# Norming inside the transposition: a diagonal tile of the tokens' factors in place of the identity

## What is computed

```
def rms_norm(x, gain):
    x32 = x.astype(jnp.float32)
    y = x32 * lax.rsqrt(jnp.mean(x32 * x32, axis=-1, keepdims=True) + RMS_EPS)
    return (y * gain.astype(jnp.float32)).astype(x.dtype)

mem_n = rms_norm(mem, mem_norm_gain)
for layer in range(DEPTH):
    hn = rms_norm(x, g[0]);  ...  x = x + rms_norm(y, g[1])
    y = memory_cross_attention(rms_norm(x, g[2]), mem_n, ...);  x = x + rms_norm(y, g[3])
    y = swiglu_ffn(rms_norm(x, g[4]), ...);  x = x + rms_norm(y, g[5])
```

## Time and profile before

| | us |
|---|---|
| median of three executions | 1306.91 |
| the profiled execution | 1306.6 |
| its span (first to last instruction) | 1304.8 |
| TensorE busy | 1286.3 (99%) |
| VectorE busy | 882.3 (68%) |
| ScalarE busy | 688.1 (53%) |
| GpSimd busy | 110.7 (8%) |

### The profile page before, as it was taken

How to read it: one execution, slowest core, us unless ns; L and a number is a source line. 1 busy time by engine, 2 the same in 40 slices (tenths; PEclk the granted TensorE clock), 3 DMA queues, 4 the chain that set the end, 5 groups by cost and what they waited for, 6 DMA issues and landing times.

```text
span 1304.8 us, 17684 instructions
## 1 busy us (share of the span) xinstructions
PE 1286.3 (99%) x7313; PEld 1108.8 (85%) x7313; DVE 882.3 (68%) x1035; ACT 688.1 (53%) x960; POOL 110.7 (8%) x176
## 2 busy tenths in 40 slices
PE   7999999999999999999999999999999999999999
PEld 6889897988888888888888888898877888888887
DVE  4566664776666767876576666768785566787775
ACT  4655554644444665564554444565556654654453
POOL 7200100100000100030100000101330003000000
PEclk9999999999999999999999999999999999999999
DMA  8754653555555543454355555553444445465552
GB/s 261 245 168 138 193 179 99 192 195 186 186 191 193 182 163 119 151 174 149 126 189 195 187 187 184 182 195 106 161 136 155 155 136 187 136 198 190 193 194 97
DMA packets 156113, 223.64 MB, mean 171 GB/s; under 512 B 6103, under 2 KB 107635, under 8 KB 156032
## 3 DMA queue, kind: packets, MB, share of 16 engines
q1 hardware_dynamic: 154240, 218.18, 50.1%
q0 software_dynamic: 1664, 4.27, 1.1%
q10 hardware_dynamic: 128, 0.05, 0.0%
HBM read 221.44 MB, written 1.05 MB: 171 GB/s over the span
## 4 chain that ended last, share of the span: by engine, by line
PE 91%; DVE 4%; ACT 3%; POOL 1%; issue 1%; DMA 1%; SPq 0%; POOLq 0%; ACTq 0%
PE ps L403 18%; PE ps L453 9%; PE ps L405 9%; PE ps L455 9%; PE ps L454 9%; PE ps L388 5%; PE ps L389 5%; PE ps L390 5%; PE ps L588 4%; PE ps L590 4%; PE ps L589 4%; DVE wlo L1671 1%; PE ps L475 1%; PE ps L901 1%; ACT whi L1131 1%; PE ps L523 1%
## 5 line engine op out<-in xcount | busy, mean ns | idle before, releaser
L1671 DVE TENSOR_TENSOR wlo<-raw,whi 128x1024 fp32r<-128x1024 f32 x411 | 493.0, 1229 | 171.2 <-ACT whi L1131 168.4
L1131 ACT ACTIVATE whi<-raw 128x1024 fp32r<-128x1024 f32 x412 | 425.4, 1052 | 341.5 <-PE ps L403 156.1
L403 PE MATMUL ps<-RR,whi 128*128 128x512 f32 x1024 | 353.7, 396 | 0.7 <-DVE ar L1774 0.7
L405 PE MATMUL ps<-RR,wlo 128*128 128x256 f32 x1024 | 264.8, 279 | 0.1
L453 PE MATMUL ps<-whi,RR 128*128 128x512 f32 x592 | 238.0, 402 | 1.6 <-DVE RR L1945 0.4
L455 PE MATMUL ps<-whi,RR 128*128 128x512 f32 x592 | 231.0, 390 | 0.0
L454 PE MATMUL ps<-wlo,RR 128*128 128x512 f32 x592 | 230.9, 390 | 0.0
L403 PEld LDWEIGHTS ps<-RR,whi 128*128 128x128 f32 x1024 | 184.8, 188 | 36.3 <-DVE ar L1774 0.9
L405 PEld LDWEIGHTS ps<-RR,wlo 128*128 128x128 f32 x1024 | 193.0, 188 | 11.8 <-DVE RR L1701 0.4
L388 PE MATMUL ps<-RR,whi 128*128 128x256 f32 x512 | 147.4, 288 | 1.7 <-DVE RR L1701 1.3
L389 PE MATMUL ps<-RR,whi 128*128 128x256 f32 x512 | 144.8, 283 | 0.0
(11 more groups left out here) (337 smaller groups left out, 1275.4 us busy)
## 6 DMA issues: line engine op xcount, KB each, us to landing
raw<-in_ffn_w_gate_up SPq DMA_DIRECT2D x44, 1024.0 KB, 5.0
raw<-in_ffn_w_down SPq DMA_DIRECT2D x33, 1024.0 KB, 4.8
raw<-in_w_in SPq DMA_DIRECT2D x28, 1024.0 KB, 4.9
raw<-in_ffn_w_up SPq DMA_DIRECT2D x22, 1024.0 KB, 5.1
raw<-in_xa_w_kv SPq DMA_DIRECT2D x16, 1024.0 KB, 5.2
raw<-in_sb_w_qkv SPq DMA_DIRECT2D x12, 1024.0 KB, 5.0
raw<-in_ml_w_in SPq DMA_DIRECT2D x11, 1024.0 KB, 7.6
raw<-in_xa_w_q SPq DMA_DIRECT2D x8, 1024.0 KB, 5.3
```

Source lines behind the costliest of these rows:

```text
L403: m = pe.matmul(two(ps[:, bank, :]), p.hi[:, k, :], XT2[:, k, :, :], start=k == 0, stop=k == 7)
L405: pe.matmul(ps[:, bank, 0:256], p.lo[:, k, :], X.h[:, k, :], start=False, stop=False)
L1131: act.activation(p.hi, p.raw, ACT.Copy).then_inc(S["w_hi"], 1)
L1671: dve.tensor_tensor(p.lo, p.raw, p.hi.bitcast(F32), ALU.subtract).then_inc(S["w_lo"], 2 if p.n == 2 else 1)
```

## The change

The row tile is no longer multiplied. VectorE multiplies the 128 by 128 identity by the 128 factors of the row tile instead, which gives a diagonal tile `dg[:, t, :]`, in norms of tokens and of memory. TensorE then multiplies the raw rows (`xr`, or `mem_tm` for the memory) by that diagonal tile in a plain matmul: the result is the transposed block, each token's column scaled by its factor. The position of every instruction in every engine's program is the same; its operands, and on TensorE its kind, change. GpSimd's reload of `mem_tm` with the second memory now waits until the last low parts of the first memory's transposed rows are written, since TensorE reads `mem_tm` itself.

```diff
+        dg = sb("dg", [128, NT, 128])
...
+            def scaled_tile(src, t, k, b, half):
+
+                return pe.matmul(ps[:, b, 256 * half + 128 * t:256 * half + 128 * t + 128], src[:, t, 128 * k:128 * k + 128],
+                                 dg[:, t, :], start=True, stop=True, skip_group_check=True)
+
             def norm_rows(no):
 
-                turn(xn, 8, "n_x", (2 * no + 1, 2 * no + 2), (0, 1, 2, 3), "n_T")
+                for t in range(NT):
+                    pe.wait_ge(S["n_x"], 2 * no + t + 1)
+                    for k in range(8):
+                        m = scaled_tile(xr, t, k, *half_bank(k, (0, 1, 2, 3)))
+                        if t:
+                            m.then_inc(S["n_T"], 1)
                 return Rows(XTh, XTl, S["n_lo"], [8 * no + k + 1 for k in range(8)])
 
             def mem_rows(i, part):
 
-                turn(mem_n[i][:, :, 512 * part:512 * part + 512], 4, "m_x", (2 * i + 1, 2 * i + 2), (6, 7), "m_T")
+                for t in range(NT):
+                    pe.wait_ge(S["m_x"], 2 * i + t + 1)
+                    for k in range(4):
+                        m = scaled_tile(mem_tm, t, 4 * part + k, *half_bank(k, (6, 7)))
+                        if t:
+                            m.then_inc(S["m_T"], 1)
...
-                    pe.transpose(ps[:, b, 256 * half + 128 * t:256 * half + 128 * t + 128], xn[:, t, 128 * k:128 * k + 128],
-                                 ident[:, :]).then_inc(S["n_T"], 1)
+                    scaled_tile(xr, t, k, b, half).then_inc(S["n_T"], 1)
...
-                    dve.tensor_scalar(xn[:, t, :], xr[:, t, :], n_st[no][t][2], None, ALU.mult).then_inc(S["n_x"], 1)
+                    dve.tensor_scalar(dg[:, t, :], ident[:, :], n_st[no][t][2], None, ALU.mult).then_inc(S["n_x"], 1)
...
-                    dve.tensor_scalar(mem_n[i][:, t, :], mem_tm[:, t, :], m_st[i][t][2], None, ALU.mult).then_inc(S["m_x"], 1)
+                    dve.tensor_scalar(dg[:, t, :], ident[:, :], m_st[i][t][2], None, ALU.mult).then_inc(S["m_x"], 1)
...
-            pool.wait_ge(S["m_x"], 2)
+            pool.wait_ge(S["m_lo"], 8)
             for t in range(NT):
                 pool.dma_start(mem_tm[:, t, :], m2[:, t, :]).then_inc(S[f"mem1_in{t}"], 16)
```

## The result

The changed kernel takes 1322.04 us (median of four runs, 1321.57 to 1322.60), the kernel before 1306.92 us on the same chip (1306.78 to 1306.99). The ratio is 1.0113 with a 95% interval of 1.0101 to 1.0125: +15.1 us, where the forecast was +16.7 and the range +13.6 to +19.6. The profiled execution took 1321.57 us, 15.0 more than that of the kernel before (1306.6).

The account below looks back on a forecast made before the run. TensorE, busy 1286.3 of 1304.8 us, was taken as the bound. Norms 1 to 6 +10.8, memory +3.6, norm 7 +1.8, norm 0 +1.8, waits -0.9 and -0.45 gave +16.7: 1323.6 us, range 1320.5 to 1326.5.

Parts of the forecast that it names:

- The price of a block: On TensorE, a plain fp32 product takes 0.217 us where a transposition took 0.104: 0.113 us extra per block.
- The rule of a factor of four: Skill's rule that fp32 transposing is four times faster: 0.416 us per product, 50 us added; weighed and not followed.
- Nothing hides it: At norms 1 to 6 and the memory rows, TensorE's extra goes straight into the span: +10.8 and +3.6 us.
- The rival of hidden turns at norms 3, 5 and 6: TensorE has slack where the chain leaves it, so 5.4 us of 48 blocks vanish: 1319.1 us; chance 4%.
- Norm 0: At the start, the 22nd record comes later at the low clock, delaying ScalarE's first read to about 11.9: +1.8 us (1.4 to 2.2).
- the rival that counted 0.5 us for it: Products cost no more than transpositions, leaving only gains, 0.5 us of them at norm 0: 1305.1 us; chance 3%.
- VectorE's gift: VectorE's tiles take 0.24 us, each 0.5 us shorter; waits go at norms 3 and 6 (-0.9 us) and norm 7 (-0.45 us).
- The sum: All terms over the whole kernel: 10.8 + 3.6 + 1.8 + 1.8 - 0.9 - 0.45 = +16.7 us.
- The rival of a relief that outweighs: A product's second record runs in the first's drain, so blocks cost no more: -1.8 us, 1305.1 us; chance 3%.

Follow-up runs that it names:

- The half alone: The kernel before with TensorE's part only: VectorE still multiplies the rows, the 160 blocks are plain fp32 products by the identity; 1323.38 us, ratio 1.0124.
- the dose: The changed kernel with each of the 160 products issued twice into the same place; 1356.57 us, ratio 1.0376.
- the fp32r kernel: The changed kernel with the diagonal tile written as fp32r and used as both operands of the 160 products; 1306.36 us, ratio 0.9995.
- VectorE's half alone: The kernel before with VectorE making diagonal tiles, while TensorE transposes the raw rows with the identity; 1304.38 us, ratio 0.9981.
- the last experiment: The changed kernel with VectorE's copies at norms 3, 5 and 6 moved behind the first four low parts; 1322.29 us, ratio 1.0117.
- the last version of the kernel before: The kernel before with VectorE's copies at norms 3, 5 and 6 behind all eight low parts, norm 7's rows multiplied in halves; 1305.17 us, ratio 0.9990.

## Why the prediction was right, and what was mis-sized

1. *The price of a block.* Right in kind and size: 0.217 expected, 0.218 measured; extra 0.114 us in the turns of 16 against 0.113, from the rows of three lines that had nothing to do with norms. One reading in it is an average: within a turn the transpositions start 0.109 us apart and the records of products 0.112, and 0.104 and 0.109 come out because the matmul behind the last one starts 0.03 us after it. That short end is the same on both sides, so the difference holds. The half alone, the dose and the fp32r kernel show it: two records in place of one, 0.109 us each. The rule of a factor of four (the Trainium skill, "TensorE: Matmul & The Clock Gate", Terms) is refuted for this shape: 3.49 / 1.66 = 2.1.
2. *Nothing hides it.* Right: the stretches between the turns are unchanged to 0.06 us except where a wait of VectorE ended. The rival of hidden turns at norms 3, 5 and 6 fails: each grew by 1.8 us in full, and what came back there, 0.5 to 0.7 us, is less than a turn's growth.
3. *Norm 0.* The step is off: "What the end of this step hangs on is ScalarE's first read at 10.62, which needs ... the 11th of all" and the +1.8 us drawn from it. The 22nd record does set the read after the change, but the clock rose within the turn, so it came sooner: the read is at 11.63, not at 12.4, and the term was 1.0 us in the profile and 1.2 us by medians.

```profile
11.63 0.84 ACT L1178 ACTIVATE RR<-ps,gcol 128x256 fp32r<-128x256 f32 x2 [0.95 <-PE ps L483]
...
13.07 0.39 PE L389 MATMUL ps<-RR,whi 128*128 128x256 f32 x1 [0.42 <-DVE RR L1716]
```

   Before the change the read was held at least as much by ScalarE's own weight piece: with products put ahead of norm 0 the turn was done 1.1 us sooner, and the read still began at 10.60. For the same reason VectorE's lead of 0.5 us is worth 0.1 us where TensorE keeps its transpositions, and the rival that counted 0.5 us for it had too much.
4. *VectorE's gift.* Undersized. The tile takes 0.286 us, not 0.24. The listed waits, 0.45 and 0.42 us, were taken for the whole loss at norms 3 and 6; the ledger shows 0.7 and 0.7, because a wait is counted from the end of the matmul before, and TensorE could have started sooner than that. Here the matmul at 444.07 ends at 444.46 and 0.45 us of wait follow, but its neighbours stand 0.23 us apart, so 0.60 us are lost, and 0.11 more behind it, where the next two starts are 0.22 us apart in place of 0.11 (two pieces of the timeline of the kernel before, norm 3 and norm 5):

```profile
443.84 0.39 PE L454 MATMUL ps<-wlo,RR 128*128 128x512 f32 x1
444.07 0.39 PE L455 MATMUL ps<-whi,RR 128*128 128x512 f32 x1
...
656.51 0.39 PE L403 MATMUL ps<-RR,whi 128*128 128x512 f32 x1
656.74 0.33 PE L405 MATMUL ps<-RR,wlo 128*128 128x256 f32 x1
656.90 0.39 PE L403 MATMUL ps<-RR,whi 128*128 128x512 f32 x1
657.38 0.39 PE L405 MATMUL ps<-RR,wlo 128*128 128x256 f32 x1
```

   Norm 5 has no listed wait and gave back 0.5 us: its product at 657.38 starts 0.48 us after the one before where 0.23 is usual, too little to show as idle, and smaller ones lie around it. My -0.9 us for this term, with nothing for norm 5, was -1.9. Norm 7's -0.45 was -0.47.
5. *The sum.* The turns were 0.2 us dearer than worked out, norm 0 0.8 us cheaper, the gifts 1.0 us larger: 16.7 + 0.2 - 0.8 - 1.0 = 15.1. That this lies in the range is in part luck. The ends that I worked out were 15.4 and 18.7, and +15.1 is below the lower one, since norm 0 (1.0, against 1.4 to 2.2) and the gifts (2.4, against 0.5 to 1.8) both left their bounds. It is inside only because I had widened the range to 13.6, and I did that towards hidden turns, which is not what happened.
6. *The rival of a relief that outweighs.* It needed an extra per block below 0.011 us. What speaks for it is true (VectorE's half alone is faster than before), but only with transpositions or with one-record products.

What stays open is what sets the moment at which the clock rises at the start. It moves norm 0's term by as much as the difference between my 1.8 and the measured 1.2: in the last experiment, whose start is that of the changed kernel, the clock rose at 11.5 us in place of 10.4, and the first turn of the memory came 0.65 us later (64.27 in place of 63.62). No experiment here controls it. In the two kernels with work put ahead of norm 0 it rose at 8.8 and 8.7 us, earlier than in any of the other eleven profiles (10.1 to 17.2), with one profile each.

## What to carry to other kernels

Folding a factor into a matmul that has to run anyway is free only if the matmul needs no more records than before: here a transposition of fp32 was one record and the product that replaced it two, and the engine that paid was the full one. With fp32r operands it was one record, and the cost was gone. Price it by the distance of starts of the same shape elsewhere in the trace. And when an engine is late, look first for what can stand behind the late work in its own queue: moving a copy of 0.68 us at three places and halving a multiplication got 1.85 us of the 2.6 that VectorE's half of the change was worth, without its cost. Where the copy goes decides it: behind four of the eight low parts it gained little, behind all eight it did.

## What the runs showed of the hardware

**The clock at the start.** In every profile TensorE began with records of 128 columns 0.213 us apart, and at some point they closed up to 0.109 to 0.112 (products of 256 columns, from 0.213 to 0.12): the clock's two levels, 1.2 and 2.4 GHz. The granted clock reads 1.00 on both sides, so the spacing has to be read, not that column. The packed trace shows why: its first record of the granted clock begins where the spacing closes up (12.53 us in the kernel before, 10.39 in the changed one, 17.30 in the last version of the kernel before), there is none ahead of it, and the column reads 1.00 where there is no record. The point is not the same for each execution. It lay at 10.4 us in the changed kernel, 11.7 in that of identity products, 15.4 in that of fp32r products, and 17.2 in the last version of the kernel before, where three products in a row look so:

```profile
16.82 0.41 PE L388 MATMUL ps<-RR,whi 128*128 128x256 f32 x1
17.03 0.41 PE L389 MATMUL ps<-RR,whi 128*128 128x256 f32 x1
17.24 0.31 PE L390 MATMUL ps<-RR,wlo 128*128 128x256 f32 x1
17.39 0.28 PE L388 MATMUL ps<-RR,whi 128*128 128x256 f32 x1
17.51 0.28 PE L389 MATMUL ps<-RR,whi 128*128 128x256 f32 x1
```

That execution took 1306.90 us, while seven of its eleven took 1305.08 to 1305.17. Its ledger puts 1.8 us of loss between 12 and 62 us, which is that difference. The other slower ones were not profiled; that their clock rose late as well is likely, not shown.

**The clock rose behind transpositions alone.** In the kernel of raw transposed rows TensorE had done nothing but transpositions when the records closed up at 10.1 us. In these windows at its start

```profile
9.12 0.85 PE L483 MATMUL ps<-ident,xr 128*128 128x128 f32 x3
...
9.76 0.56 PE L483 MATMUL ps<-ident,xr 128*128 128x128 f32 x2
...
10.15 0.49 PE L483 MATMUL ps<-ident,xr 128*128 128x128 f32 x3
```

three records last 0.85 us and later 0.49. The rule of the Trainium skill that I had weighed in the prediction ("TensorE: Matmul & The Clock Gate", Part 4: PE-mode transpose: transpositions don't count as work for the clock) is not borne out here.

**The shortest distance.** At the higher clock the starts of records with 128 columns stood 0.109 us (transposition), 0.112 us (plain fp32, each of two) and 0.112 us (fp32r) apart, though fp32r records of 256 columns need only 0.12. In the fp32r kernel the loads of the stationary tile, one for each record, stand 0.11 us apart in norm 1's turn as well, and the first two products of that turn only 0.057. That the loads set the distance is likely, not shown.
